# First norm and its modulation taken tile by tile: a new order of the first loads and of the work of five engines

## The reference, cut to what matters

```python
def modulate(x, shift, scale):
    return rms(x) * (1 + scale[:, None]) + shift[:, None]
...
    mod = jax.nn.silu(c) @ p['w_ada'] + p['b_ada']
    mod_c = (jax.nn.silu(c_ctx) @ p['w_ada'] + p['b_ada'])[None]
    sh1, sc1, g1, sh2, sc2, g2 = jnp.split(mod, 6, axis=-1)
...
    h = modulate(x, sh1, sc1)
    hc = modulate(cx, csh1, csc1)
    na, mla, sg, gqa = token_mixing_inputs(h, p, pos)   # z = h @ p['w_in']
```

## Time and profile before

| what | value |
|---|---|
| median of 3 runs | 2370.47 us (2367.01 to 2371.37) |
| the profiled execution's own time | 2370.61 us |
| its span in the profile | 2368.9 us |
| PE busy, share of the span | 2278.4 us, 96% |
| DVE busy | 1348.6 us, 57% |
| ACT busy | 937.4 us, 40% |
| POOL busy | 164.8 us, 7% |
| mean granted TensorE clock | 0.992 |

### The profile page before, as it was taken

One profiled execution on the slowest core, in us unless ns is written; L12 is line 12 of the kernel. 1 busy time (PEld: TensorE's weight loads), 2 busy tenths in 40 slices (PEclk: granted clock), 3 DMA queues, 4 the chain that ended last, 5 costly groups with the idle time before them and its releaser, 6 DMA issues.

```text
span 2368.9 us, 35088 instructions
## 1 busy us (share of the span) xinstructions
PE 2278.4 (96%) x12916; PEld 1896.0 (80%) x12916; DVE 1348.6 (57%) x1954; ACT 937.4 (40%) x1381; POOL 164.8 (7%) x169
## 2 busy tenths in 40 slices
PE   6999988999999999999999999999999998999999
PEld 6788766788888878888888876776788878888887
DVE  6555566476667475425534566556745566645545
ACT  3454556522223243213312345546643334423332
POOL 2113010000000000000000002220100000000000
PEclk9999999999999999999999999999999999999999
DMA  7112110244343311111111131121045552222223
GB/s 284 45 54 72 36 40 19 72 156 138 133 142 133 124 54 62 62 63 63 62 62 63 62 117 63 63 71 32 36 144 176 175 178 78 101 98 92 94 98 115
DMA packets 58625, 221.26 MB, mean 93 GB/s; under 512 B 6720, under 2 KB 6720, under 8 KB 57872
## 3 DMA queue, kind: packets, MB, share of 16 engines
q1 hardware_dynamic: 44496, 160.46, 19.5%
q0 software_dynamic: 14016, 59.26, 7.1%
HBM read 214.45 MB, written 5.24 MB: 93 GB/s over the span
## 4 chain that ended last, share of the span: by engine, by line
PE 86%; DVE 6%; ACT 3%; issue 3%; DMA 1%; PEldq 0%; SPq 0%; PEld 0%; DVEq 0%; ACTq 0%
PE PS L611 83%; PE PS L903 3%; DVE TM L1459 1%; ACT W_hi L1081 1%; DVE XY L1459 1%; ACT TM L1081 1%; DVE H_lo L1459 1%; DVE ROPE L1512 1%; DVE W_lo L1456 1%; ACT XY L1081 1%; DVE F_lo L1456 1%; DMA ROPE<-w_mod 1%; ACT F_hi L1081 0%; DMA XY<-x_in 0%; ACT H_hi L1081 0%
## 5 line engine op out<-in xcount | busy, mean ns | idle before, releaser
L611 PE MATMUL PS<-H_hi,W_hi 128*128 128x512 f32 (+1 forms) x2256 | 689.3, 358 | 25.0 <-DVE H_lo L1459 9.6
L611 PE MATMUL PS<-H_hi,W_lo 128*128 128x512 f32 (+1 forms) x2256 | 678.7, 354 | 0.0
L611 PE MATMUL PS<-H_lo,W_hi 128*128 128x512 f32 (+1 forms) x2256 | 676.3, 353 | 0.0
L1456 DVE TENSOR_TENSOR W_lo<-W_st,W_hi 128x1024 fp32r<-128x1024 f32 x278 | 343.5, 1237 | 569.3 <-ACT W_hi L1081 567.8
L1081 ACT ACTIVATE W_hi<-W_st 128x1024 fp32r<-128x1024 f32 x278 | 293.7, 1057 | 838.8 <-PE PS L611 829.1
L611 PEld LDWEIGHTS PS<-H_hi,W_hi 128*128 128x128 f32 x2256 | 377.1, 189 | 102.9 <-issue 30.5
L611 PEld LDWEIGHTS PS<-H_lo,W_hi 128*128 128x128 f32 x2256 | 374.5, 189 | 61.3 <-issue 2.7
L611 PEld LDWEIGHTS PS<-H_hi,W_lo 128*128 128x128 f32 x2256 | 375.2, 189 | 59.1
L611 PE MATMUL PS<-F_hi,W_hi 128*128 128x512 f32 (+1 forms) x968 | 296.2, 355 | 13.5 <-DVE XY L1459 5.1
L611 PE MATMUL PS<-F_hi,W_lo 128*128 128x512 f32 (+1 forms) x968 | 295.3, 354 | 0.0
L611 PE MATMUL PS<-F_lo,W_hi 128*128 128x512 f32 (+1 forms) x968 | 293.3, 352 | 0.0
(11 more groups left out here) (129 smaller groups left out, 2086.9 us busy)
## 6 DMA issues: line engine op xcount, KB each, us to landing
W_st<-w_all SPq DMA_DIRECT2D x278, 512.0 KB, 3.5
RA<-w_mod POOLq DMA_DIRECT2D x40, 512.0 KB, 3.7
TM<-w_mod POOLq DMA_DIRECT2D x40, 512.0 KB, 3.7
RA<-w_ada SPq DMA_DIRECT2D x8, 512.0 KB, 8.7
XY<-bias_na POOLq DMA_DIRECT2D x2, 1792.0 KB, 7.3
RA<-w_mod SPq DMA_DIRECT2D x6, 512.0 KB, 8.2
XY<-x_in SPq DMA_DIRECT2D x4, 768.0 KB, 11.5
x_spill<-XY POOLq DMA_DIRECT2D x1, 3072.0 KB, 11.1
```

The source lines that it names most:

```text
L611: return nc.tensor.matmul(o, lhsT, rhs, start=start, stop=stop)
L1456: return nc.vector.tensor_tensor(o, a, b, f)
```

## The change

- **Loads.** SP issues scale tile 0, then all four quarters of x, weight blocks 0 and 1, and after that the other scale and shift tiles by a list (`FIRST_LOADS`). The waits on slots stay the same.
- **Sum of squares.** POOL's six adds are gone. PE multiplies the matrix of ones with each of the eight squares as it comes (`sq_pass`), in bank pair 3, for all 768 columns; ACT's squares wait for PE.
- **Root.** One root for all 768 columns. Ahead of it DVE makes the scale sums of tiles 0 and 1 and splits weight blocks 0 and 1; ACT loads its table and splits the blocks.
- **Shift.** Tile j of the shift is now 8 matmuls with `CC` as the stationary side (2 columns) and 128 columns of the weight tile moving (`shift_rows`), a copy of the 2x128 result to SBUF by ACT (`shift_row`), one small matmul that turns it into columns (`shift_columns`), and an add by DVE (`shift`).
- **Norm.** It goes feature tile by feature tile over both halves. In step k DVE takes the shift of tile k, the products of tile k, the low parts of tile k-1, and then the scale sums of tile k+2. PE takes in step k the shift rows of tile k+2, the shift column of tile k+1, and then the matmuls of both column tiles for feature tile k.

The diff, cut; lines that it takes out of `ada_tile`, `ada`, `squares_of_x` and the three `first_norm` stand in the kernel above and are left out here.

```diff
+def first_norm_counts():
+
+    return dict(sq=KT, y0=1, y_sq=1, newton=2, norm_u=2 * KT, norm_hi=2 * KT, norm_lo=2 * KT)
+
+
+FIRST_LOADS = (("scale", 0), ("x", 0), ("x", 1), ("x", 2), ("x", 3), ("w", 0), ("w", 1), ("scale", 1), ("scale", 2),
+               ("shift", 0), ("scale", 3), ("shift", 1), ("scale", 4), ("shift", 2), ("scale", 5), ("shift", 3),
+               ("scale", 6), ("shift", 4), ("scale", 7), ("shift", 5), ("shift", 6), ("shift", 7))
+AHEAD = 2
...
+        SH_ROW = [TT[0:2, P * i:P * i + P] for i in range(2)]
...
-            for j in range(KT):
-                if j >= 3:
-                    sp.wait_ge(S["scale_acc"], 2 * (j - 2))
-                sp.dma_start(SCALE_W[j % 3], w_mod[SC1 + j]).then_inc(scale_loaded[j % 3], 16)
-                if j >= 3:
-                    sp.wait_ge(S["ada_used"], j - 2)
-                sp.dma_start(SHIFT_W[j % 3], w_ada[j]).then_inc(shift_loaded[j % 3], 16)
-                if j < KT // 2:
+            for what, j in FIRST_LOADS:
+                if what == "scale":
+                    if j >= 3:
+                        sp.wait_ge(S["scale_acc"], 2 * (j - 2))
+                    sp.dma_start(SCALE_W[j % 3], w_mod[SC1 + j]).then_inc(scale_loaded[j % 3], 16)
+                elif what == "shift":
+                    if j >= 3:
+                        sp.wait_ge(S["ada_used"], j - 2)
+                    sp.dma_start(SHIFT_W[j % 3], w_ada[j]).then_inc(shift_loaded[j % 3], 16)
+                elif what == "x":
                     k = 2 * T * j
                     sp.dma_start(XY[:, k:k + 2 * T], x_in[:, k:k + 2 * T]).then_inc(x_loaded[j], 16)
+                else:
+                    sp.dma_start(W_st[:, j, :], w_all[IN_BLOCKS[j]]).then_inc(w_loaded[j], 16)
...
-            for k in range(1, KT - 1):
-                pool.wait_ge(S["sq"], k + 1)
-                wait(pool, "sq_sum", k - 1)
-                nc.gpsimd.tensor_tensor(TT, SQ[0] if k == 1 else TT, SQ[k % 2], ALU.add).then_inc(S["sq_sum"], 1)
...
+            def shift_rows(j):
+
+                pe.wait_ge(shift_loaded[j % 3], 16 * (j // 3 + 1))
+                wait(pe, "sh_row", j - 1)
                 for k in range(KT):
+                    ins = mm(bank(4 + j % 2)[0:2, 0:P], CC[:, k, :], SHIFT_W[j % 3][:, P * k:P * k + P], k == 0,
+                             k == KT - 1)
+                ins.then_inc(S["ada_used"], 1)
+
+            def shift_columns(j):
+
+                pe.wait_ge(S["sh_row"], j + 1)
+                pe.wait_ge(S["newton"], 1)
+                wait(pe, "sh_add", j - 1)
+                mm(bank(6 + j % 2)[:, 0:2], SH_ROW[j % 2], MT[0:2, M_ID, 0:2], True, True).then_inc(S["sh_tr"], 1)
...
+                pe.wait_ge(S["const_loaded"], 16)
+                for k in range(KT):
+                    pe.wait_ge(S["sq"], k + 1)
+                    for s0, sn in segs(T):
+                        ins = mm(pair(3)[:, s0:s0 + sn], MT[:, M_ONE, :], SQ[k % 2][:, s0:s0 + sn], k == 0, k == KT - 1)
+                    ins.then_inc(S["sq_pass"], 1)
+                pe.wait_ge(S["silu_c"], 1)
+                shift_rows(0)
+                shift_rows(1)
+                shift_columns(0)
+                for k in range(KT):
+                    if k + 2 < KT:
+                        shift_rows(k + 2)
+                    if k + 1 < KT:
+                        shift_columns(k + 1)
+                    for t in range(2):
+                        if k == 0:
+                            have_block(t)
+                        pe.wait_ge(S["norm_hi"], 2 * k + 2)
+                        pe.wait_ge(S["norm_lo"], 2 * k + 2)
+                        ins = gemm_k(t, T, t, k, KT, H_hi, H_lo)
+                        if k == KT - 1:
+                            ins.then_inc(S["block_done"], 1)
+                base.advance(**first_norm_counts())
...
-                two_early_tiles(T, b0, 0, l > 0)
+                if l:
+                    two_early_tiles(T, b0, 0)
...
+            def square_of_x(k):
+                act.wait_ge(x_loaded[k // 2], 16)
+                wait(act, "sq_pass", k - 1)
+                op(SQ[k % 2], X3[:, k, :], ACT.Square).then_inc(S["sq"], 1)
+
+            def shift_row(j):
+                act.wait_ge(S["ada_used"], j + 1)
+                wait(act, "sh_tr", j - 1)
+                op(SH_ROW[j % 2], bank(4 + j % 2)[0:2, 0:P], ACT.Copy).then_inc(S["sh_row"], 1)
...
+            def first_norm():
+                for k in range(KT):
+                    square_of_x(k)
+                act.wait_ge(S["eps_set"], 1)
                 load_root_table()
+                for b in range(2):
+                    split_hi(b, b, 16)
+                act.wait_ge(S["sq_pass"], KT)
+                op(NY0, pair(3, T), ACT.Abs_reciprocal_sqrt, bias=EPSB).then_inc(S["y0"], 1)
+                act.wait_ge(S["y0"], 1)
+                op(NRT, NY0, ACT.Square).then_inc(S["y_sq"], 1)
+                shift_row(0)
+                shift_row(1)
+                for k in range(KT):
+                    for h, (s0, sn) in enumerate(halves(T)):
+                        act.wait_ge(S["norm_u"], 2 * k + h + 1)
+                        op(H_hi[:, k, s0:s0 + sn], NU[k % 3][:, s0:s0 + sn], ACT.Identity,
+                           bias=MOD[:, stream(s0), SH1 + k:SH1 + k + 1]).then_inc(S["norm_hi"], 1)
+                    if k + 2 < KT:
+                        shift_row(k + 2)
+                base.advance(**first_norm_counts())
...
+            def scale_sums(j):
+                dve.wait_ge(scale_loaded[j % 3], 16 * (j // 3 + 1))
+                for c in range(2):
+                    if j == 0:
+                        dve.wait_ge(S["cb_silu"], c + 1)
+                    wait(dve, "scale_acc", 2 * j + c)
+                    nc.vector.tensor_tensor_reduce(SCALE_P, SCALE_W[j % 3], CB[c], 1.0, 0.0, ALU.mult, ALU.add,
+                                                   MOD[:, c, SC1 + j:SC1 + j + 1]).then_inc(S["scale_acc"], 1)
+
+            def scales(j0, j1):
+
                 dve.wait_ge(S["adab_loaded"], 16)
+                dve.wait_ge(S["scale_acc"], 2 * j1)
                 for c in range(2):
+                    m = MOD[:, c, SC1 + j0:SC1 + j1]
+                    tt(m, m, ADAB[:, SC1 + j0:SC1 + j1], ALU.add).then_inc(S["mod_step"], 1)
+                n_mod[0] += 2
                 dve.wait_ge(S["mod_step"], n_mod[0])
+                m = MOD[:, :, SC1 + j0:SC1 + j1]
+                nc.vector.tensor_scalar(m, m, 1.0, -0.5, ALU.add, ALU.mult).then_inc(S["mod_step"], 1)
+                n_mod[0] += 1
+                dve.wait_ge(S["mod_step"], n_mod[0])
+
+            def shift(j):
+                dve.wait_ge(S["sh_tr"], j + 1)
+                m = MOD[:, :, SH1 + j:SH1 + j + 1].rearrange("p c a -> p (c a)")
+                tt(m, bank(6 + j % 2)[:, 0:2], ADAB[:, SH1 + j:SH1 + j + 1].to_broadcast([P, 2]), ALU.add
+                   ).then_inc(S["sh_add"], 1)
...
+            def first_norm():
+                scale_sums(0)
+                for b in range(2):
+                    dve.wait_ge(w_loaded[b], 16)
+                    split_lo(b, b + 1)
+                for j in range(1, AHEAD):
+                    scale_sums(j)
+                scales(0, AHEAD)
+                m = pair(3, T)
+                dve.wait_ge(S["sq_pass"], KT)
+                dve.wait_ge(S["y_sq"], 1)
+                stt(NRT, m, EPS, NRT, ALU.add, ALU.mult).then_inc(S["newton"], 1)
+                dve.wait_ge(S["newton"], 1)
+                stt(NRT, NRT, -3.0, NY0, ALU.add, ALU.mult).then_inc(S["newton"], 1)
+                dve.wait_ge(S["newton"], 2)
+
+                def low(k):
+                    for h, (s0, sn) in enumerate(halves(T)):
+                        dve.wait_ge(S["norm_hi"], 2 * k + h + 1)
+                        stt(H_lo[:, k, s0:s0 + sn], NU[k % 3][:, s0:s0 + sn],
+                            MOD[:, stream(s0), SH1 + k:SH1 + k + 1], H_hi[:, k, s0:s0 + sn].bitcast(F32),
+                            ALU.add, ALU.subtract).then_inc(S["norm_lo"], 1)
+
+                for k in range(KT):
+                    shift(k)
+                    wait(dve, "norm_lo", 2 * (k - 2))
+                    for s0, sn in halves(T):
+                        stt(NU[k % 3][:, s0:s0 + sn], X3[:, k, s0:s0 + sn],
+                            MOD[:, stream(s0), SC1 + k:SC1 + k + 1], NRT[:, s0:s0 + sn], ALU.mult, ALU.mult
+                            ).then_inc(S["norm_u"], 1)
+                    if k:
+                        low(k - 1)
+                    if k + AHEAD < KT:
+                        scale_sums(k + AHEAD)
+                        scales(k + AHEAD, k + AHEAD + 1)
+                low(KT - 1)
+                base.advance(**first_norm_counts())
...
-                    ada()
-                    one_plus_scale(SC1)
+                    first_norm()
                 end(dve, "dve")
-                if l == 0:
-                    for b in range(2):
```

(59 more changed lines are left out.)

43 lines of the change are left out of this document (4 added, 39 removed).

## The result

The changed kernel takes 2398.7 us in the median of 4 executions (2393.5 to 2406.6), the kernel before 2370.6 us in 4 on the same chip: a ratio of 1.0119, 95% interval 1.0098 to 1.0140, so 28 us slower. The profiled execution took 2393.45 us at a mean granted clock of 0.990, 22.8 us more than that of before.

The account below looks back on a forecast made before the run. The prediction took TensorE, busy 96%, to bound the kernel: 16.7 us won ahead of the products, about 36 us lost in the loop and turn-over, so 2370.6 + 18.9 = 2389.5 us, range 2375 to 2399 us.

Parts of the forecast that it names:

- the ring: Norm loop: DVE and TensorE wait for each other every step, 7.25 us a step; slow in part, chance 0.50.
- Block 2: TensorE's first matmul on weight block 2, forecast at 94.1 us against 75.17 before, 18.9 us later.
- The root: Start of the kernel through the last Newton step: ends at 34.4 us against 51.1 before, gaining 16.7 us.
- Step 1: Second step of the norm loop: starts slow on TensorE, takes 7.8 us, to 47.7 us.
- Step 6: Norm loop step without shift rows: 2.9 us and a projection of 3.0 us, to 82.6 us.
- Shift rows: TensorE's shift matmuls in each loop step, 16 pieces: 1.05 us warm, 1.7 slow, above that 2.1 us.
- The clock in the ring: TensorE's granted clock in the loop: falls in most steps, recovers within the step; 7.25 us a step chosen.
- The warm ring: Rival: loop at full clock throughout, steps of 6.05 us, block 2 at 86.7 us, +11.5 us, 2382 us; chance 0.22.
- the middle case: Loop step between warm 6.05 and slow 8.45 us: 7.25 us, used for steps 2 to 5.
- The turn-over: TensorE's wait between the last projection and block 2: 3.1 us, of 4.15 us before.
- Everything behind is the same: After block 2 starts (75.17 us before), the program is unchanged, so the shift of that start gives the time difference.
- slow rival: Loop at low clock throughout: steps of 8.45 us, block 2 at 102.2 us, +27 us, 2398 us; chance 0.12.

Follow-up runs that it names:

- e1_cols_first: The changed kernel with the shift column for the next step issued ahead of the later tile's shift rows on TensorE; 2381.0 us, ratio 1.0051.
- e2_short_sums: The changed kernel with the scale sums of tiles 2 to 7 taken over 64 of their 1024 columns; 2400.3 us, ratio 1.0132.
- e0_again: The changed kernel run once more, unedited; 2398.0 us, ratio 1.0107 to the kernel before.
- e4_lag: e1_cols_first with column tile 1's projection three feature tiles behind column tile 0's; 2382.0 us, ratio 1.0047.
- e8_phase_early: e4_lag with both of TensorE's phase signals moved ahead of its projection loop; 2379.2 us, ratio 1.0021.
- e5_fill: The changed kernel with three more float32 matmuls of 384 columns in each step, results unread; 2389.4 us, ratio 1.0083.
- e6_sums_by_landing: e4_lag with scale tiles loaded first and all summed ahead of the products, shift rows up to five tiles ahead, columns two; 2373.9 us, ratio 1.0013.
- e7: e6_sums_by_landing with scale tiles earlier, all summed before the root, both signals before the loop, rows of tile k+4 behind projection k; 2378.7 us, ratio 1.0020.
- e9: e7 with ACT's copy of a later shift tile's row moved behind the following feature tile's rounding; 2363.9 us, ratio 0.9974.

## Why the prediction was right, and where its terms were not

**The direction and the mechanism** held: the time is slower, DVE and PE take turns, e1_cols_first shows the ring by cutting it, and e2_short_sums shows that the sums lie beside it. Block 2 was put at 94.1 us and stands at 93.93. That closeness is partly luck, since the terms below were off in both directions and cancelled. The time, 2398.7 us, is 9.2 us above the forecast of 2389.5 and 0.3 us inside the end of the range.

- **The root** was put at 34.4 us and ended at 32.45. The eight passes ended at 24.2 us and not at 26.6: once warm they took 1.29 us each, the pitch of ACT's squares, and not 1.65. DVE's wait for the first `W_hi` was 13.50 us, not 14.9. Part of the 2 us is lost again: shift tile 2 landed at 34.76 us, 3 us sooner than in the sum, but its rows and the column took 4.2 us at the low clock and not 2.1. Step 1 started at 38.96 us against the 39.9 of the sum.
- **Step 1** took 9.10 us, not 7.8: the projection at the low clock was 4.11 us (41.38 to 45.49) and not 3.85, and the rows 2.09 us and not 1.05. Step 6 took 5.12 us and not 5.9, since its projection was warm.
- **Shift rows** is the term that was mis-sized. I took 1.05 us for 16 pieces, from pieces with a 64-column stationary side, and named 0.13 us each as the upper bound. They take 1.84 us, 0.115 us each, near the upper bound. The bound came from passes with a full stationary side, and these were the better row: warm passes took 0.107 us for each 128 columns (see the last section).
- **The clock in the ring** was put down as falling in most steps, at 1.2 us a step. In the profiled execution it fell in none of steps 2 to 5. The warm ring is 7.0 us and not 6.05: the rows' 0.8 us, and 0.15 us more for the projection. So 7.0 against 7.25 us was a nearly right sum of two wrong terms, which is luck. In e0_again three of four such steps had falls and took 8.4 to 8.6 us: that is the warm ring of 7.0 us and 1.4 to 1.6 us, near what I added for the middle case, upon a base that was 1 us too low. The median has both kinds. The Trainium skill ("TensorE: Matmul & The Clock Gate", HAM oscillation) tells of a kernel whose bursts all began slow; its waits between them, about 3 to 5 us by that section, were longer than the 2.5 us here, and the prediction left this out. In e0_again the clock fell in three steps of four, in the profiled execution of the changed kernel in none of them.
- **The turn-over** was put at 3.1 us and was 4.34 us. I had let ACT's copy follow the end of tile 0; it follows the signal of the phase, which the change had put behind the last matmul, 1.2 us later here. e4_lag and e8_phase_early show this. I had looked at the matmuls' order, and not at where the signal stood among them.
- **"Everything behind is the same"** held for the program and not quite for the time. In the profiled execution the difference grew from 18.8 us at block 2 to 22.8 us at the end. By windows of 1 us over both spans the clock fell nine times behind block 2, against eight before. A fall costs about 1.7 us (seven microseconds around one, from 345 to 352 us, read 0.76, and 0.24 × 7 us = 1.7 us), so of the 4.1 us by which the difference grew 2.4 us stay open. In the median 28 us stand against the forecast's 19, just inside the range. e5_fill came out 9 to 11 us lower with a higher mean clock, and the slower executions of the changed kernel had the lower clocks. Both point to falls in the ring, which the range held as its slow rival, as the larger part of these 9 us; the overlap of the intervals leaves the size open.

The medians of e1_cols_first, e2_short_sums and e6_sums_by_landing lie 5 to 6 us higher against before's than their block 2 does, that of e4_lag 1.7 us, those of e7 to e9 1 us. No run tells what this rests on.

## What to carry to other kernels

When work is cut into short steps between two engines, follow one step through every queue and look for what is queued behind what: each of three waits here went when one call or one pair of signals was moved on one engine (17 us by the column ahead of the rows, 12 us by the copy behind the rounding, some of it the clock's, and 4 to 5 us by the signals ahead of a loop). A wait that seems to belong to data may belong to a phase signal, so a moved block of work has to be read together with the signals around it. Sums that are hidden in such a ring are no gain when made shorter, and a loss when they are moved in front of it.
